# Queries and keys of layer two's first pair from scaled, not normalised tiles, with two more columns for mean and offset

## The reference

```python
for i in range(DEPTH):
    y = branch_a(h, ...) if i % 2 == 0 else branch_b(h, w_in_b, w_out_b)
    h = layer_norm(DEEPNORM_ALPHA * h + y, ln_g[i], ln_b[i])
return h[:, N_META:]
```

## Time and profile before

| | us |
|---|---|
| median of 3 runs | 904.96 (904.74 to 905.33) |
| the profiled execution, its own time | 904.62 |
| its span from first to last record | 902.8 |
| TensorE busy in the span | 893.6 |
| VectorE, ScalarE busy | 556.0, 429.1 |

### The profile page before, as it was taken

How to read it: one execution, slowest core, us unless ns; L and a number is a source line. 1 busy time by engine, 2 the same in 40 slices (tenths; PEclk the granted TensorE clock), 3 DMA queues, 4 the chain that set the end, 5 groups by cost and what they waited for, 6 DMA issues and landing times.

```text
span 902.8 us, 17880 instructions
## 1 busy us (share of the span) xinstructions
PE 893.6 (99%) x7182; PEld 862.2 (96%) x7182; DVE 556.0 (62%) x746; ACT 429.1 (48%) x685; POOL 62.1 (7%) x85
## 2 busy tenths in 40 slices
PE   9999999999999999999999999999999999999997
PEld 9999999999999999899999999999999999988886
DVE  6578667666765767785646464555646355545546
ACT  6556455645655344385454443535444444435421
POOL 1222033113200000000000000000000000000000
PEclk9999999999999999999999999999999999999999
DMA  9774464456442555525453534444354544454622
GB/s 344 238 237 167 154 219 139 148 166 177 155 153 105 187 187 190 184 66 212 143 187 139 181 144 163 162 145 180 139 186 139 186 144 165 156 212 162 233 94 94
DMA packets 25399, 153.05 MB, mean 170 GB/s; under 512 B 3426, under 2 KB 4210, under 8 KB 8852
## 3 DMA queue, kind: packets, MB, share of 16 engines
q1 hardware_dynamic: 21744, 142.19, 43.9%
q0 software_dynamic: 2896, 7.70, 4.2%
q10 hardware_dynamic: 724, 2.66, 0.8%
HBM read 150.36 MB, written 2.18 MB: 169 GB/s over the span
## 4 chain that ended last, share of the span: by engine, by line
PE 95%; DVE 2%; DMA 1%; ACT 1%; issue 0%; SPq 0%; DVEq 0%
PE bank L342 70%; PE bank L712 10%; PE bank L457 2%; PE bank L497 2%; DMA raw<-chunks 1%; PE bank L657 1%; PE bank L656 1%; PE bank L659 1%; PE bank L624 1%; PE bank L583 1%; PE bank L597 1%; PE bank L364 1%; PE bank L365 1%; PE bank L363 1%; DVE w_lo L1073 1%; PE bank L472 0%
## 5 line engine op out<-in xcount | busy, mean ns | idle before, releaser
L342 PE MATMUL bank<-x_hi,w_hi 128*128 128x272 f32 (+1 forms) x1472 | 425.6, 289 | 0.0
L342 PE MATMUL bank<-x_hi,w_lo 128*128 128x272 f32 (+1 forms) x1472 | 421.4, 286 | 0.0
L342 PE MATMUL bank<-x_lo,w_hi 128*128 128x272 f32 (+1 forms) x1472 | 421.3, 286 | 0.0
L1073 DVE TENSOR_TENSOR w_lo<-raw,w_hi 128x2048 fp32r<-128x2048 f32 x126 | 290.4, 2308 | 207.1 <-ACT w_hi L791 174.4
L791 ACT ACTIVATE w_hi<-raw 128x2048 fp32r<-128x2048 f32 x114 | 217.9, 1913 | 157.0 <-PE bank L342 104.8
L342 PEld LDWEIGHTS bank<-x_hi,w_hi 128*128 128x128 f32 x1472 | 277.4, 188 | 1.1 <-issue 0.2
L342 PEld LDWEIGHTS bank<-x_hi,w_lo 128*128 128x128 f32 x1472 | 277.4, 188 | 0.0
L342 PEld LDWEIGHTS bank<-x_lo,w_hi 128*128 128x128 f32 x1472 | 277.0, 188 | 0.0
L342 PE MATMUL bank<-og_hi,w_hi 128*128 128x272 f32 x240 | 70.1, 292 | 0.0
L342 PE MATMUL bank<-og_hi,w_lo 128*128 128x272 f32 x240 | 69.4, 289 | 0.0
L342 PE MATMUL bank<-og_lo,w_hi 128*128 128x272 f32 x240 | 69.1, 288 | 0.0
(11 more groups left out here) (246 smaller groups left out, 1020.0 us busy)
## 6 DMA issues: line engine op xcount, KB each, us to landing
raw<-chunks SPq DMA_DIRECT2D x128, 1024.0 KB, 4.8
work<-bias_table POOLq DMA_DIRECT2D x8, 512.0 KB, 5.6
work<-chunks SPq DMA_DIRECT2D x4, 512.0 KB, 11.5
...
```

The source lines that it names most:

```text
L342: last = mm(o, l, r, start=(kt == 0 and n == 0), stop=(kt == KT - 1 and n == 2))
L1073: V.tensor_tensor(lo_part, raw[:, half, :, :], hi_part.bitcast(f32), ALU.subtract) \
```

## The change

1. `x_hi` and `x_lo` get two columns more: gain and offset of the layer norm (split in hi and lo once, in layer one).
2. In the output projection ScalarE makes `x_hi` = gain times the tile that is not yet normalised (`scaled_hi`), and VectorE its remainder (`scaled_rest`), for all 16 tiles. There is no `AHEAD`; all weights go into their regular places, P_B + 1's second half after the last output projection. In `out_a` the split of the next weights comes first and the second split last but for the remainders, in every pair.
3. The first queries and keys run on these tiles at once, with 258 and 274 columns. The two dummy series, `on_tokens` and the spreading of the root are gone; mean and mean square of all tokens (`statistics`) are made after the second feature tile, at full width.
4. VectorE then centres and scales as before (from rows in SBUF, two tiles at a time), ScalarE applies gain and offset to `x_hi` and to `h` (`normal`), VectorE makes `x_lo` (`rest`), each pair after the queries and keys have used the old tiles (`step_done`). The values' projection waits for them pair by pair.
5. Queries and keys are corrected when they leave PSUM: `unfold` on VectorE (four instructions, four times), one more on ScalarE with the offset. They stand before the last two pairs.
6. The first weights come as one transfer and are rounded in one instruction.

The slots of the weights are renumbered. The core of the diff (longer runs of removed lines are left out; they stand in the kernel above):

```diff
-x_hi = sb("x_hi", [128, KT, T], f32r)
-x_lo = sb("x_lo", [128, KT, T], f32r)
+x_hi_all = sb("x_hi", [128, KT, T + 2], f32r)
+x_lo_all = sb("x_lo", [128, KT, T + 2], f32r)
+x_hi, x_lo = x_hi_all[:, :, 0:T], x_lo_all[:, :, 0:T]
 og_hi = sb("og_hi", [128, KT, T], f32r)
...
         for m in KV_ORDER[n]:
-            if m == 0:
-                for c in range(2):
-                    sp.dma_start(kv_raw[:, 0, c, :], chunks[0][:, c * CW:(c + 1) * CW]) \
-                      .then_inc(first_loaded[c], 16)
-                continue
             if m < len(KV_PARTS):
...
                 if kt == 0 and not banks:
                     pe.wait_ge(tile_free[u], P if free_at is None else free_at)
+                if x_pairs and u == 0 and kt % 2 == 0:
+                    pe.wait_ge(x_lo_ready, x_pairs + kt // 2 + 1)
...
+    def statistics():
+        pe.wait_ge(c_summed, KT)
+        mm(mean_rows, mean_w[:], ln["c_sum"], start=True, stop=True)
+        pe.wait_ge(sq_summed, KT)
+        mm(sq_rows, mean_w[:], ln["sq_sum"], start=True, stop=True).then_inc(mean_ready, 1)
     def queries_and_keys_0():
+        pe.wait_ge(consts_ready, 4)
+        pe.wait_ge(o_read, O_A)
+        pe.wait_ge(pt_copied, PT_A)
+        pe.wait_ge(gb_lo, 1)
         for half in range(2):
             for k in range(HALF):
                 kt = half * HALF + k
                 tiles = []
                 for pair in range(2):
                     hi_part, lo_part = split_views(P_B + pair, half)
-                    cols, banks = ((SEQ_COLS, acc), (ALL, k_acc_0))[pair]
+                    cols, banks = ((slice(META, T + 2), acc), (slice(0, T + 2), k_acc_0))[pair]
                     for u in range(2):
                         part = slice(u * 128, u * 128 + 128)
                         tiles.append((banks[u][:, 0:cols.stop - cols.start], hi_part[:, k, part],
-                                      lo_part[:, k, part], x_hi[:, kt, cols], x_lo[:, kt, cols]))
+                                      lo_part[:, k, part], x_hi_all[:, kt, cols], x_lo_all[:, kt, cols], u))
                 if k == 0:
                     pe.wait_ge(lo_ready, 2 * (P_B + 1) + half - 3)
                 if kt == 0:
-                    for u in range(2):
+                    tiles = [tiles[0], tiles[2], tiles[3], tiles[1]]
+                pe.wait_ge(x_lo_ready, X_A + kt + 1)
+                for n, (o, whi, wlo, xh, xl, u) in enumerate(tiles):
+                    if kt == 0 and n % 3 == 0:
                         pe.wait_ge(tile_free[u], P_B)
...
+                    mm(o, whi, xh, start=(kt == 0), stop=False)
+                    mm(o, whi, xl, start=False, stop=False)
+                    last = mm(o, wlo, xh, start=False, stop=(kt == KT - 1))
                     if kt == KT - 1:
-                        last.then_inc(tile_full[n % 2], 1)
+                        last.then_inc(tile_full[u], 1)
                     if kt == HALF - 1 and n % 2:
                         last.then_inc(half_used, 1)
-                    elif kt < HALF - 1 and n == 1:
-                        last.then_inc(first_step, 1)
+                    elif kt % 2 and kt < KT - 1 and n == 3:
+                        last.then_inc(x_used, 1)
+                if kt == 1:
+                    statistics()
...
         project(P + 2, x_hi, x_lo, ALL, between=lambda: scores_b(i),
-                banks=v_acc_0 if isinstance(i, int) else None, layer_b=True)
+                banks=v_acc_0 if isinstance(i, int) else None, layer_b=True,
+                x_pairs=X_A + KT if isinstance(i, int) else None)
...
-    if 2 * n >= HALF:
-        eng.wait_ge(*((first_step, 2 * n - HALF + 3) if 2 * n < 2 * HALF - 2 else (half_used, P_B + 1)))
+    if n == HALF // 2 - 1:
+        eng.wait_ge(half_used, P_B + 2)
+    elif n == HALF - 1:
+        eng.wait_ge(tile_full[1], P_B + 2)
+    else:
+        eng.wait_ge(x_used, n + 1 - n // (HALF // 2))
...
         A(dst[:], flat[:, lo:lo + n], ACT.Copy).then_inc(consts_ready, 1)
+    act.wait_ge(consts_loaded, 16 * 3)
+    A(x_hi_all[:, :, T:T + 2], ln_gb.rearrange("p a k -> p k a"), ACT.Copy).then_inc(gb_hi, 1)
     for u in range(2):
...
+    def scaled_hi(t):
+        A(x_hi[:, t, :], h[:, t, :], ACT.Identity, scale=ln_gb[:, 0, t:t + 1]).then_inc(x_hi_ready, 1)
     for u in range(2):
         square(0, u, c_ready, u + 1)
-    for n in range(6):
+        scaled_hi(u)
+    for n in range(7):
         P = P_OUT_A + 1 + n
         split_hi(P + 2, 0)
-        if P >= P_B - 3:
-            split_hi(P + 2, 1)
         for u in range(2):
             square(2 + 2 * n, u, tile_free[u], P + 1)
-        if P < P_B - 3:
-            split_hi(P + 2, 1)
-    for half in range(2):
-        split_hi(P_B + 1, half)
+            scaled_hi(2 + 2 * n + u)
+        split_hi(P + 2, 1)
+    guess_rstd(ln["rstd"], ln["var"], ln_step, 4, 0)
+    def normal(n):
+        step_done(act, n)
+        act.wait_ge(normed, n + 1)
+        for t in (2 * n, 2 * n + 1):
+            gain, bias = (ln_gb[:, m, t:t + 1] for m in range(2))
+            A(x_hi[:, t, :], h[:, t, :], ACT.Identity, bias=bias, scale=gain).then_inc(x_hi_ready, 1)
+            act.wait_ge(x_hi_ready, X_A + KT + t + 1)
+            A(h[:, t, :], h[:, t, :], ACT.Identity, bias=bias, scale=gain).then_inc(h_offset, 1)
+    for n in range(6):
+        normal(n)
+        if n in (2, 4):
+            split_hi(P_B + 2, (n - 2) // 2)
     for u in range(2):
...
+        act.wait_ge(folds_scaled, u + 1)
+        A(b["q"][:, u, :], b["w"][:, u * SEQ:(u + 1) * SEQ], ACT.Identity, bias=fold[:, u, 1:2], scale=-1.0) \
+            .then_inc(tile_free[u], 1)
+    for u in range(2):
+        act.wait_ge(folds_scaled, u + 3)
+        k, bias = b["sp"][:, u * T:(u + 1) * T], fold[:, 2 + u, 1:2]
+        if u:
+            A(b["kT"][:, T:T + META], k[:, SEQ:T], ACT.Identity, bias=bias, scale=-1.0)
+        A(b["kT"][:, B_KEYS[u]] if u else b["kT"][:, 0:T], k[:, 0:SEQ if u else T], ACT.Identity, bias=bias,
+          scale=-1.0).then_inc(tile_free[u], 1)
+    for n in (6, 7):
+        normal(n)
...
     first_raw, first_hi, first_lo = kv_views(0)[0]
-    for c in range(2):
-        dve.wait_ge(first_loaded[c], 16)
-        V.tensor_copy(first_hi[:, c, :], first_raw[:, c, :]).then_inc(kv_first, 1)
+    dve.wait_ge(kv_loaded[0], 16)
+    V.tensor_copy(first_hi, first_raw).then_inc(kv_first, 1)
     x_rest(0)
-    dve.wait_ge(kv_first, 2)
+    dve.wait_ge(kv_first, 1)
...
     split_lo(4, 0)
+    dve.wait_ge(gb_hi, 1)
+    V.tensor_tensor(x_lo_all[:, :, T:T + 2], ln_gb.rearrange("p a k -> p k a"),
+                    x_hi_all[:, :, T:T + 2].bitcast(f32), ALU.subtract).then_inc(gb_lo, 1)
...
+    def scaled_rest(t):
+        dve.wait_ge(x_hi_ready, X_A + t + 1)
+        V.scalar_tensor_tensor(x_lo[:, t, :], h[:, t, :], ln_gb[:, 0, t:t + 1], x_hi[:, t, :].bitcast(f32),
+                               ALU.mult, ALU.subtract).then_inc(x_lo_ready, 1)
     def out_a(P, t):
-        if P >= P_B - 3:
-            split_lo(P + 2, 0)
-        for u in range(2):
-            if u and P == P_B - 2:
-                split_lo(P_B, 1)
+        split_lo(P + 2, 0)
+        for u in range(2):
             combined(P, u, t + u)
-            if u == 0 and P < P_B - 3:
-                split_lo(P + 2, 0)
-            if u and P == P_B - 3:
-                split_lo(P + 2, 1)
             dve.wait_ge(tile_free[u], P + 1)
             V.tensor_tensor(ln["c_sum"], ln["c_sum"], h[:, t + u, :], ALU.add).then_inc(c_summed, 1)
             dve.wait_ge(c_summed, t + u + 1)
-            prepared(t + 2 + u)
-        if P < P_B - 3:
+            if P < P_B - 1:
+                prepared(t + 2 + u)
+        for u in range(2):
+            squared(t + u, u)
+        if P < P_B - 1:
             split_lo(P + 2, 1)
         for u in range(2):
-            squared(t + u, u)
+            scaled_rest(t + u)
...
         squared(u, u)
-    for n in range(6):
+        scaled_rest(u)
+    for n in range(7):
         out_a(P_OUT_A + 1 + n, 2 + 2 * n)
...
     def newton(y, v, tmp, step, at):
...
+    V.tensor_copy(ln["mu"], mean_rows).then_inc(mu_copied, 1)
     dve.wait_ge(mu_copied, 1)
-    V.tensor_tensor(ln["m2"], ln["tmp"], ln["tmp"], ALU.mult).then_inc(ln_step, 1)
+    V.tensor_tensor(ln["m2"], ln["mu"], ln["mu"], ALU.mult).then_inc(ln_step, 1)
     dve.wait_ge(ln_step, 3)
...
+    V.scalar_tensor_tensor(ln["var"], sq_rows, EPS, ln["m2"], ALU.add, ALU.subtract).then_inc(ln_step, 1)
+    split_lo(P_B + 1, 1)
     dve.wait_ge(ln_step, 4)
     dve.wait_ge(rs_guess, 2)
     newton(ln["rstd"], ln["var"], ln["tmp"], ln_step, 4)
-    dve.wait_ge(mean_ready, 4)
+    def on_pair(row):
+        return row.rearrange("p (a t) -> p a t", a=1).to_broadcast([128, 2, T])
+    def centre(n):
+        hh = h[:, 2 * n:2 * n + 2, :]
+        V.tensor_tensor(hh, hh, on_pair(ln["mu"]), ALU.subtract).then_inc(rows_centred, 1)
+    def scaled(n):
+        hh = h[:, 2 * n:2 * n + 2, :]
+        dve.wait_ge(rows_centred, n + 1)
```

(32 more changed lines are left out.)

138 lines of the change are left out of this document (24 added, 114 removed).

## The result

The change makes the kernel slower: 917.18 us median of 4 runs (916.58 to 918.29) against 904.93 (904.74 to 905.33) for the kernel before on the same chip, ratio 1.0136 with a 95% interval of 1.0123 to 1.0148. The profiled execution took 917.2 us; its span is 915.3 us (before 902.8), so 12.5 us are to be found.

A forecast was written before the change was run, and what follows sets the result against it. TensorE, busy 99% of the span, was taken as the bound. Output projection +1.5, layer two up to the next pair +3.9 and start -0.2 summed to +5.2 us: 910.1 against the median of 904.96, range 905.6 to 913.0.

The forecast's parts named there:

- Part 3: Layer two, from the statistics to the next pair: VectorE's chain runs late and TensorE waits, +9.2 us.
- Part 1: First step of the output projection: TensorE waits for the residual add behind the weights' split, +1.5 us.
- Part 2: Start of layer two: queries and keys no longer wait for the normalisation, so the hole closes, -5.3 us.
- Part 4: Kernel start: one weight transfer in place of two may land the second weights earlier, -0.2 us.
- ScalarE needs as much (four by 0.415 ...): Layer two's normalisation: ScalarE needs 1.92 us a pair of tiles, as much as VectorE's 1.9.
- the value copy only as a wait of the turning behind it: Behind the tails in layer two: TensorE waits 2.6 us for VectorE's value copy for the second head.
- The later waits: Before layer two's next pair: TensorE waits 2.1 us for ScalarE's exponentials and value copies, 1.7 for the gate.
- Rival "clock": Layer two's new waits: TensorE's clock falls to 1.2 GHz, slowing the next half projection; 915.8 us, chance 4%.
- Rival "stride": Matmuls reading the 274-wide x tiles: each takes 0.42 ns longer, 1.9 us in all; 912.0 us, chance 9%.

The follow-up runs named there:

- e6: Changed kernel with VectorE adding the first tile's product before the weights' split in the output projection's first step; 915.45 us, ratio 1.0107.
- e4: Changed kernel with 34 matmuls that nothing reads put into TensorE's wait ahead of the gate projection; 916.63 us, ratio 1.0127.
- e1: Kernel before with its rows' tiles (both halves) laid out 274 columns apart instead of 272; 907.66 us, ratio 1.0027.

## Why the prediction was wrong

The direction and the place were right, the size was not: 910.1 with at most 913.0, against 917.18. The step that failed is Part 3, with the pitch, which the sum put at nothing. Step by step:

- **Part 1** (+1.5): the wait is there, 1.6 us at the place named, and the stretch grew by 1.8 (e6 took all of it back). Right.
- **Part 2** (-5.3): the values start 24.6 us behind the output projection (378.89 to 403.51), as worked out. Right.
- **Part 4** (-0.2): -0.13 by the profile, and not shown to be the change's.
- **Part 3** (+9.2) is where the forecast fails. It put the next pair at 3.9 us behind its old distance from the end of layer one; it was 8.2. One term was mis-sized and two were left out. First, "ScalarE needs as much (four by 0.415 ...)": that is the turn of an instruction that takes only an offset from memory. The new ones take gain and offset both:

```profile
390.13 0.61 ACT L933 ACTIVATE h<-h,ln_gb 128x272 f32<-128x272 f32 x1
390.65 0.60 ACT L931 ACTIVATE x_hi<-h,ln_gb 128x272 fp32r<-128x272 f32 x1
```

  They take 0.61 us, turn in 0.52 and make a pair of 2.32 instead of 1.92. The capping came at 423.22, where my distances give 421.0: 2.2 us. I put them down to this pair: 0.8 of them arise in the last two pairs of rows, which follow one another at ScalarE's pace, and most of the others are VectorE's waits for ScalarE in the first ones (0.62, 0.32 and 0.32). No run gave these instructions the old turn, so the 2.2 are read from the timeline. The Trainium skill ("ScalarE: Activation LUTs", the section "What ACT_TABLE_LOAD costs", on the speed of ACTIVATE) says that each per-partition pointer operand adds about 93 ns; by that rule, the trace agrees: 0.51 with one and 0.61 with two. Second, the forecast let TensorE begin the gate projection where the values ended, and had the value copy only as a wait of the turning behind it. The accumulator that this copy frees is the gate's. In my own numbers the values ended at 416.5 and the copy came some 7 us later, so the wait could have been read from them. The later waits, which had been counted, then fell away; what is left for this step is the remainder of the sum below, 0.6 us. Third, the clock.
- **Rival "clock"** (4%, 915.8) was real, priced on a wait of 2 to 2.6 us; the wait was 5.17, and fifteen matmuls behind it took 0.094 us each more, 1.4 us (e4 took back 0.8). The Trainium skill ("TensorE: Matmul & The Clock Gate", Part 1) ties the lower level to an idle engine; the trace agrees for this wait.
- **Rival "stride"** (9%, +1.9) was real as well: 0.42 ns per matmul was put, the traces have 0.42 to 0.57 against the kernel before, 2.1 us in all (e1 2.35). That the rival's price came near is partly luck: with the small half in the same place the pitch costs 1.1 ns, and the move of that half gave 0.6 back. I gave it nothing, "since no row shows any". But no row could have shown it, so that was no reason for zero, and the term belonged in the range.
- What is left is 0.6 us in layer one, where a transfer of raw weights took 8.55 us instead of 7.97. It took 8.1 to 8.6 in the other runs whose chain shows it, some of them with the instructions of the kernel before, so it is not shown to be the change's.

Together, for the profiled execution, whose span grew by 12.5 us where 5.2 were forecast: 2.2 for ScalarE's pair, 2.1 for the pitch, 1.4 for the clock, 0.6 for the transfer, 0.3 more than forecast in the output projection and 0.1 at the start make 6.7 of the 7.3 us. The remaining 0.6 lie between the last residual add and the next pair; I put them down to the gate's wait, and no run isolates them. Two mechanisms that I treated as exclusive rivals of the forecast came on top of it, which is why the range did not hold.

VectorE's timeline read as a chain of its own gives the direction at once, but not the size. In the kernel before it has one gap of 4.9 us between the last work of the normalisation and the gates' weights. Counted from the last residual add, the change starts that chain 5.0 us later (3.8 before, 8.8 after) and adds 4.5 us of unfolding. Against 4.9 us of slack that is 4.6, near my 3.9; the gates' weights came 7.7 later and the next pair 8.2. The missing 3 us are VectorE's waits for ScalarE in this stretch (5.7 us, where the kernel before has 0.3), less what VectorE's shorter pairs of rows save (1.9 us each instead of 2.3). So the chain has to be read over both engines.
